# Expert projections of a mixture of experts: weights as the moving operand in plain float32, biases by matmul

## The reference, cut to what matters

```
logits = xt @ w_router + b_router            # 32 experts
top_v, top_i = top_k(logits, 4); gates = softmax(top_v)
# for every expert e, on the rows that chose it:
hdn  = xblk @ w1[e] + b1[e]                  # 1024 -> 2048
gate = minimum(hdn[:, :1024], 7.0)
lin  = clip(hdn[:, 1024:], -7.0, 7.0)
act  = gate * sigmoid(1.702 * gate) * (lin + 1.0)
yb   = act @ w2[e] + b2[e]                   # 1024 -> 1024
out[token] += gate_weight * yb
```

## Time and profile before

| what | value |
|---|---|
| median of three runs | 2697.32 us |
| span of the profiled execution | 2696.2 us |
| TensorE matmul busy | 2443.9 us (91%) |
| TensorE weight load busy | 1888.3 us (70%) |
| VectorE busy | 954.6 us (35%) |
| ScalarE busy | 631.2 us (23%) |
| mean granted TensorE clock | 0.941 |

### The profile page before, as it was taken

The page is one execution under the profiler, slowest core; times in us unless marked ns, Lnnn a source line. Parts: engine busy times, 40 slices in busy tenths (PEclk is TensorE's granted clock), DMA queues, the critical chain, the costliest instruction groups (busy, mean ns, idle before and its releaser), DMA issues. The chain is left out here.

```text
span 2696.2 us, 36055 instructions
## 1 busy us (share of the span) xinstructions
PE 2443.9 (91%) x14394; PEld 1888.3 (70%) x14394; DVE 954.6 (35%) x1243; ACT 631.2 (23%) x822; POOL 254.4 (9%) x179
## 2 busy tenths in 40 slices
PE   5799889987957899997899999999999999999991
PEld 3455456464725444475899999999999999999981
DVE  3332314464556000003133433434334243343335
ACT  3422203041322100001122322323223222232231
POOL 0000020324042000000000000000000000000000
PEclk8899899998976899996899999999999999999996
DMA  5111022313121422232588888888888888888854
GB/s 165 49 47 47 0 94 67 119 49 110 78 93 47 151 71 73 77 125 96 193 325 307 320 319 317 322 313 320 324 309 319 315 319 329 303 320 320 313 196 167
DMA packets 160137, 527.75 MB, mean 196 GB/s; under 512 B 15382, under 2 KB 81848, under 8 KB 124248
## 3 DMA queue, kind: packets, MB, share of 16 engines
q1 hardware_dynamic: 152808, 505.69, 51.8%
q0 software_dynamic: 7280, 21.37, 2.6%
HBM read 510.12 MB, written 21.10 MB: 197 GB/s over the span
## 5 line engine op out<-in xcount | busy, mean ns | idle before, releaser
L1619 PE MATMUL ps<-temps,weights 128*128 128x96 f32 x8192 | 925.2, 276 | 0.0
L1619 PEld LDWEIGHTS ps<-temps,weights 128*128 128x128 f32 x8192 | 920.9, 193 | 0.0
L1683 DVE TENSOR_TENSOR w_low<-weights,w_high 128x1024 fp32r<-128x1024 f32 x256 | 305.1, 1223 | 52.5 <-ACT w_high L1677 52.4
L1631 DVE TENSOR_TENSOR temps<-ps,b1T 128x768 f32<-128x768 f32 x64 | 58.4, 954 | 671.9 <-PE ps L1619 671.9
L1677 ACT ACTIVATE w_high<-weights 128x1024 fp32r<-128x1024 f32 x256 | 260.4, 1053 | 48.8 <-PE ps L1694 48.8
L1609 ACT ACTIVATE temps<-ps 128x384 f32<-128x384 f32 x66 | 28.9, 491 | 795.5 <-PE ps L1601 795.5
L1694 PE MATMUL ps<-w_high,act_high 128*96 128x512 f32 x512 | 204.2, 399 | 8.9 <-DVE w_low L1683 8.9
L1694 PE MATMUL ps<-w_high,act_low 128*96 128x512 f32 x512 | 201.5, 394 | 0.0
L1694 PE MATMUL ps<-w_low,act_high 128*96 128x512 f32 x512 | 200.8, 392 | 0.0
L1242 PE MATMUL ps<-weights 128*128 128x512 f32 x384 | 169.0, 600 | 5.1 <-PEq L1145 5.1
L850 PE MATMUL ps<-weights 128*128 128x512 f32 x384 | 169.7, 597 | 0.0
(11 more groups left out here) (280 smaller groups left out, 2248.8 us busy)
## 6 DMA issues: line engine op xcount, KB each, us to landing
weights<-in_w SPq DMA_DIRECT2D x384, 1024.0 KB, 5.8
weights<-in_w_in SPq DMA_DIRECT2D x32, 1024.0 KB, 5.4
weights<-in_w_in SPq DMA_DIRECT2D x16, 512.0 KB, 5.1
temps<-cum_rows SPq DMA_DIRECT2D x8, 1024.0 KB, 7.1
weights<-cum_rows SPq DMA_DIRECT2D x8, 1024.0 KB, 11.2
weights<-in_w_up_ssd SPq DMA_DIRECT2D x8, 1024.0 KB, 6.5
weights<-expert_rows SPq DMA_DIRECT2D x16, 512.0 KB, 10.0
ssd_out_T<-temps SPq DMA_DIRECT2D x4, 1024.0 KB, 3.9
```

The costliest lines, as they stand in the source:

```text
L1619: last = nc.tensor.matmul(ps[:, m // 4, (m % 4) * CAP:(m % 4 + 1) * CAP], slot(k, 1)[:, 0, m * P:(m + 1) * P], xeT[:, k, :], start=k == 0 ...
L1631: nc.vector.tensor_tensor(dst.rearrange("p (a c s) -> p a c s", a=2, c=4), ps[:, 2 * i:2 * i + 2, 0:4 * CAP].rearrange("p a (c s) -> p a c ...
L1683: nc.vector.tensor_tensor(w_lo[:, cols], src, w_hi[:, cols].bitcast(F32), ALU.subtract).then_inc(w_lo_ok, 1)
```

## The change

Both projections now use the transposed rows or activations (96 columns) as stationary operand and stream 512 columns of weights in plain float32. The splits of w2 and of the activations are gone, with their buffers. The hidden layer now has rows on partitions, so the bias differs along the free axis; it enters by four float32r matmuls of `pick` (a 0/1 matrix that selects row e and row 32 + e) with `b1_s` (b1's rounded part in rows 0 to 31, the rest in rows 32 to 63, zeros below). Activations need a transpose of their own (`acts_pe`). Sigmoid and product become one Silu with scale 1.702, and the factor 1/1.702 goes into a copy. The weights' store becomes one ring of 8 slots (`RING`) through which the 12 tiles of a pass go in the order of use. Index matmuls are float32r with two columns, four in place of eight, and stand inside the up projection. Gathered rows have two buffers, and slots and gathers run a pass further ahead.

```
-            for k in range(NK):
-                pe.wait_ge(exp_w[k], it * 16 + 16)
-                for m in range(2 * DFF // P):
-                    last = nc.tensor.matmul(ps[:, m // 4, (m % 4) * CAP:(m % 4 + 1) * CAP], slot(k, 1)[:, 0, m * P:(m + 1) * P], xeT[:, k, :], ...
-                last.then_inc(l1_used, 1)
+        def up_pe(pe, it, odd):
+            pe.wait_ge(x_ok, it + 1)
+            pe.wait_ge(pick_ok, it + 1)
+            if not is_first(it):
+                pe.wait_ge(gl_ok, it * 2)
+            for n in range(4):
+                nc.tensor.matmul(ps[0:CAP, n, :], pick[:, :], b1_s[:, n * 512:(n + 1) * 512], start=True, stop=False)
+            for k in range(UP):
+                at = ring_at(it, odd, k)
+                pe.wait_ge(exp_w[at], landed(it, odd, k))
+                for n in range(4):
+                    last = nc.tensor.matmul(ps[0:CAP, n, :], xT[:, k, :], slot(at, 1)[:, 0, n * 512:(n + 1) * 512], start=False, stop=k == UP - 1)
+                last.then_inc(w_used, 1)
+                if k == 2:
+                    if not is_first(it):
+                        pe.wait_ge(a_ok, it)
+                    slots_pe(pe, it + 2)
+        def slots_pe(pe, it):
+            pe.wait_ge(s_oh, it + 1)
+            for t in range(NT):
+                last = nc.tensor.matmul(ps[0:CAP, 6, 400:402], sel[:, t, :], slot_of[:, bass.ds((it % NE) * NT * 2 + t * 2, 2)], ...
+            last.then_inc(ix_ps, 1)
+        def gate_dve(v, it):
+            v.wait_ge(w_used, tile_no(it, UP - 1) + 1)
+            if not is_first(it):
+                v.wait_ge(aT_tp, it)
+            nc.vector.tensor_scalar(g_w[0:CAP, :]..., ps[0:CAP, 0:2, :], LIMIT, None, ALU.min).then_inc(gl_ok, 1)
+            nc.vector.tensor_scalar(l_w[0:CAP, :]..., ps[0:CAP, 2:4, :], LIMIT, -LIMIT, ALU.min, ALU.max).then_inc(gl_ok, 1)
+        def silu_act(act, it):
+            act.wait_ge(gl_ok, it * 2 + 1)
+            nc.scalar.activation(g_w[0:CAP, :], g_w[0:CAP, :], ACT.Silu, scale=ALPHA).then_inc(silu_ok, 1)
+        def glu_dve(v, it):
+            v.wait_ge(silu_ok, it + 1)
+            v.wait_ge(gl_ok, it * 2 + 2)
+            nc.vector.scalar_tensor_tensor(l_w[0:CAP, :], l_w[0:CAP, :], 1.0, g_w[0:CAP, :], ALU.add, ALU.mult).then_inc(glu_ok, 1)
+        def acts_pe(pe, it):
+            pe.wait_ge(glu_ok, it + 1)
+            pe.wait_ge(x_ok, it + 2)
+            for c in range(NK):
+                last = nc.tensor.transpose(ps[:, 6 + c // 4, ...], l_w[0:CAP, c * P:(c + 1) * P], ident[0:CAP, 0:CAP])
+            last.then_inc(aT_tp, 1)
+        def acts_act(act, it):
+            act.wait_ge(aT_tp, it + 1)
+            nc.scalar.activation(a_f[:, :]..., eighths(6), ACT.Copy, scale=1.0 / ALPHA).then_inc(a_ok, 1)
+        def down_pe(pe, it, odd, first):
+            pe.wait_ge(a_ok, it)
+            if not (isinstance(it, int) and it == 1):
+                pe.wait_ge(ye_ok, it - 1)
+            for u in range(DOWN):
+                at = ring_at(it, odd, first + u)
+                pe.wait_ge(exp_w[at], landed(it, odd, first + u))
+                for k in (2 * u, 2 * u + 1):
+                    for n in range(2):
+                        last = nc.tensor.matmul(ps[0:CAP, 4 + n, :], aT[:, k, :], slot(at, 2)[:, k % 2, n * 512:(n + 1) * 512], ...
+                last.then_inc(w_used, 1)
+        def pass_pe(pe, it, odd):
+            up_pe(pe, it, odd)
+            rows_pe(pe, it + 1, 1 - odd)
+            if not is_first(it):
+                down_pe(pe, it, odd, UP)
+            acts_pe(pe, it)
+        def pass_act(act, it):
+            if not is_first(it):
+                acts_act(act, it - 1)
+                if not (isinstance(it, int) and it == 1):
+                    down_act(act, it - 1, TILES, it * 16 - 32)
+            rows_act(act, it + 1)
+            silu_act(act, it)
+        def pass_dve(v, it):
+            if not is_first(it):
+                places_dve(v, it - 1)
+            tokens_dve(v, it + 2)
+            slots_dve(v, it + 3)
+            pick_dve(v, it + 1)
+            gate_dve(v, it)
+            glu_dve(v, it)
+        def load_tile(sp, it, odd, j):
+            sp.wait_ge(w_used, tile_no(it, j) - (RING - 1))
...
```

Here `down_pe(pe, it, ...)` in the new code works on the expert of pass it - 1. In the blocks before: the merge block loses the load, the four transposes (L1312) and the copy (L1371) of b1 and the preload of w2; the routing block gains two loads of b1, and these instructions (the first of them in VectorE's chain, the last three at its end):

```
+                then(nc.vector.tensor_copy(slots4[:, :, :, 0], tok_id.unsqueeze(2).broadcast_to([P, NT, NE])))
+                nc.scalar.activation(b1_s[0:2 * NE, :], b1_rows[0:2 * NE, :], ACT.Copy).then_inc(b1_hi, 1)
+                nc.vector.tensor_tensor(expert_at, ident[:, 0:NE], ident[:, NE:2 * NE], ALU.add).then_inc(b1_lo, 1)
+                nc.vector.memset(b1_s[2 * NE:P, :].bitcast(F32), 0.0).then_inc(b1_lo, 1)
+                nc.vector.tensor_tensor(b1_s[low_half, :], b1_rows[low_half, :], b1_s[low_half, :].bitcast(F32), ALU.subtract).then_inc(b1_lo, 1)
```

More of the change, by code:

```diff
@@ L49 @@
 FAR = 4096.0
+RING = 8
 UNIT = 2048
@@ L1378, in build, with sb_r @@
         rt_ps = sem("rt_ps")
-        take_anew()
+        b1_in = sem("b1_in")
+        b1_hi = sem("b1_hi")
+        b1_lo = sem("b1_lo")
+        before_experts.close()
+        def sb_r(name, cols):
+            return ctx.enter_context(nc.sbuf_tensor(name, [P, cols], F32R))
+        x_f, a_f = (sb(n, NK * CAP) for n in ("rows_T", "act_T"))
+        b1_s = sb_r("bias_split", 2 * DFF)
+        pick = sb_r("pick", CAP)
+        slot_of = sb_r("slot_of", 2 * NE * NT)
+        sel_r = sb_r("sel", NT * CAP)
+        take_anew()
+        gate = take(NT * TOPK).rearrange("p (t k) -> p t k", t=NT)
+        rank_m = take(NT * NE)
+        iota_r = take(SLOTS + CAP)
+        trips = take(2).bitcast(I32)
+        expert_at = take(NE)
+        after_route = used["main"]
         top_v = take(NT * 8).rearrange("p (t k) -> p t k", t=NT)
@@ L1400, in build @@
         trips_f = take(1)
-        trips = take(2).bitcast(I32)
-        after_route = used["main"]
+        assert used["main"] <= TEMPS - NT * D
         with nc.Block() as block:
@@ L1407, in _ @@
                 sp.dma_start(b2_w[0:NE, :], b2).then_inc(b_in, 16)
+                for half in range(2):
+                    sp.dma_start(b1_rows[half * NE:(half + 1) * NE, :], b1).then_inc(b1_in, 16)
             @block.gpsimd
@@ L1604, in rows_act @@
+            last.then_inc(xT_tp, 1)
         def rows_act(act, it):
-            act.wait_ge(xeT_ps, it + 1)
+            act.wait_ge(xT_tp, it + 1)
             if not is_first(it):
[L1607 to L1613, removed]
-            if not is_first(it):
-                pe.wait_ge(b1_add, it * 2)
-            for k in range(NK):
-                pe.wait_ge(exp_w[k], it * 16 + 16)
-                for m in range(2 * DFF // P):
-                    last = nc.tensor.matmul(ps[:, m // 4, (m % 4) * CAP:(m % 4 + 1) * CAP], slot(k, 1)[:, 0, m * P:(m + 1) * P], xeT[:, k, :],
-                                            start=k == 0 and m % 4 == 0, stop=k == NK - 1, skip_group_check=True)
-                last.then_inc(l1_used, 1)
@@ L1748, in _ @@
             def _(sp):
-                last, before = last_pass(sp), pass_before(sp)
-                load_w1(sp, 1)
-                with sp.Fori(2, last + 1, 2) as pair:
-                    for it in (pair, pair + 1):
-                        load_w1(sp, it)
-                        load_w2(sp, it - 1)
-                load_w2_last(sp, before)
+                end = after_last(sp)
+                for j in range(TILES):
+                    load_tile(sp, 1, 1, j)
+                with sp.Fori(2, end, 2) as pair:
+                    for odd in range(2):
+                        for j in range(TILES):
+                            load_tile(sp, pair + odd, odd, j)
@@ L1768, in _ @@
-                scatter_pool(pool, last)
-                pool.wait_ge(xe_in, last * 16 + 32)
-                pool.wait_ge(ye_out, last * 16 + 16)
+                end = after_last(pool)
+                for it in range(4):
+                    gather_pool(pool, it, it % 2)
+                with pool.Fori(2, end, 2) as pair:
+                    for odd in range(2):
+                        scatter_pool(pool, pair + odd - 2)
+                        gather_pool(pool, pair + odd + 2, odd)
+                scatter_pool(pool, end - 2)
@@ L1792, in _ @@
+                with pe.Fori(2, end, 2) as pair:
+                    for odd in range(2):
+                        pass_pe(pe, pair + odd, odd)
+                down_pe(pe, end, 0, 0)
             @block.scalar
             def _(act):
-                last, before = last_pass(act), pass_before(act)
+                end = after_last(act)
+                before = eng_before(act)
                 rows_act(act, 0)
-                rows_act(act, 1)
-                act_act(act, 0)
+                pass_act(act, 0)
@@ L1798, in _ @@
                 pass_act(act, 1)
-                with act.Fori(2, last + 1, 2) as pair:
-                    for it in (pair, pair + 1):
-                        pass_act(act, it)
-                split_act(act, last)
```

(26 more changed lines are left out.)

289 lines of the change are left out of this document (95 added, 194 removed).

## The result

| | before | after |
|---|---|---|
| median, us | 2697.65 (2697.01 to 2700.14, 4 runs) | 2766.18 (2765.41 to 2768.09, 4 runs) |
| ratio | 1 | 1.0253, 95% interval 1.0239 to 1.0268 |
| span of the profiled execution | 2696.2 | 2766.0 |
| VectorE, ScalarE busy | 954.6, 631.2 | 601.4, 375.5 |

The change makes the kernel 68.5 us slower; the forecast was 64.2. The two profiled executions differ by 69.8 us.

What follows compares the result with a forecast made beforehand. TensorE, busy throughout the experts' stage, was taken as the bound. Start -0.6, pass 0 +3.3, thirty full steps +62.7 and last pass -1.2 gave +64.2 us, a median of 2761.5 us, range 2744 to 2786.

Steps and rivals of the forecast that it cites:

- The bound: Experts' stage: a pass lasts the sum of TensorE's pieces, 41.69 us before and 43.78 after, 2.09 more.
- Up: Up projection per pass: 64 float32 records at 0.4292 make 27.47 us, 1.17 less than 28.64.
- Down: Down projection per pass: 32 float32 records at 0.4292 make 13.73 us, 2.59 more than 11.14.
- Biases, slots, transposes: TensorE's small matmuls per pass: biases 0.98 us, slots 0.38, transposes of rows and activations 0.61 each, 1.22 together.
- Hand-overs: Activations' chain to `acts_pe`, at most 4.7 us, and other engines' work stay hidden under transposes and down of 14.3.
- `up` of pass 0: Start of the experts' stage: the edges before it add up so that it begins about 0.6 us earlier.
- the last pass: End of the experts' stage: +2.8 us before the first down ends, -4.0 after it, together -1.2.
- A: TensorE's 512-column pass needs less than 0.429 a record with 96 stationary columns; faster from 0.407 on; chance 0.03.
- B: Weights arrive late through 8 slots: with flow held to 290 GB/s, pass 45.9 us, time 2829; chance 0.05.
- C: A hand-over, chain to `acts_pe` or type switches, is exposed in each pass: at 1 us each 2793; chance 0.07.
- D: TensorE's granted clock falls under continuous 512-column streaming: at a mean of 0.95, +74, 2835 us; chance 0.03.
- E: Terms cancel because slots and biases vanish under streaming and the edges win: no change; chance below 0.01.

Runs made afterwards that it cites:

- experiment 1: Changed kernel without its four bias matmuls per pass (b1 left out): 2734.18 us, 32.0 less than the changed kernel.
- experiment 2: Kernel before with only the down projection made one plain float32 matmul, no splits: 2775.77 us, +77.4, ratio 1.0289.
- experiment 3: Kernel before with only the new index matmuls (four float32r of two columns for eight float32 of one): 2662.20 us, ratio 0.9868.
- experiment 4: Changed kernel with half of the down matmuls left out (first 512 output columns only), all loads kept: 2542.39 us.
- experiment 6: Changed kernel with its four index matmuls issued twice in each pass, same result: 2774.83 us, +8.7.
- experiment 5: Changed kernel's layout with both projections split into three float32r matmuls, activations' transposes inside the next pass: 2523.04 us, ratio 0.9354 to the kernel before.

## Why the prediction was right, step by step

**The bound.** TensorE's sum set the pass before and after. Experiments 1 to 4 and 6 each changed one term, experiment 5 several, and each distance moved by the price of what was changed: 42.87 where 42.8 was expected, 44.34 (44.2 to 44.3), 40.67 (40.7 to 40.8), 36.92 (36.92), 36.08 (36 to 37), 44.14 (43.79 + 0.33 = 44.12).

**Up.** 27.80 with slots, where 27.47 + 0.38 stood. Streaming w1 was not tried alone. After is 9.6 faster than experiment 2, which shares its down, while the new slots alone gave 36.1 (experiment 3). So the rest of the change (streamed w1, biases, transposes of activations, the work on b1, the open hand-over of pass 0) costs 36.1 - 9.6, some 26, together. By the rows, 31 x (27.47 + 0.99 + 0.61 - 28.64) = 13 of them fall in the steady passes; the split of the rest is worked out, not shown by a run.

**Down.** 13.73 to the hundredth. This is the cause of the loss: experiment 2 alone costs 77 us, and experiment 5, which returns to float32r and extends it to w1, turns the loss into a gain. The argument for 0.429 with 96 stationary columns was thinner than it reads: the block of rows 6 has fewer rows (32) but the same 128 columns as rows 5, so neither tested fewer columns. The 13.73 of after does.

**Biases, slots, transposes.** 0.99 (0.98 stood), 0.33 by the sum (0.38), and 0.66 + 0.61 (1.22). The slots came out 0.05 lower and the row transposes 0.05 higher, so that the sum meets 43.79 to 0.01 is in part luck. Experiments 1 and 6 put the net prices at 0.92 and 0.35. Two bounds of the biases were reckoned wrong: without the change of type 4 x 0.231 is 0.92, not 0.85, and 1.72 is the price of one float32 record a matmul, where rows 5 have two. The range did not hang on either.

**Hand-overs.** None shows in a steady pass. They are open only where no down hides them: the transposes of activations of pass 0 wait 4.53 (at 1335.66), the last down 1.99 (at 2698.91). In the timeline of VectorE around the end of an up projection of after, the clamps and the product are done 4.1 us after 2024.81, and the transposes that need them start at 2039.20:

```profile
2025.01 1.22 DVE L1677 TENSOR_SCALAR temps<-ps 96x1024 f32<-96x1024 f32 x1 [15.87 <-PE ps L1665]
2026.15 1.21 DVE L1678 TENSOR_SCALAR temps<-ps 96x1024 f32<-96x1024 f32 x1
2027.64 1.22 DVE L1689 SCALAR_TENSOR_TENSOR temps<-temps 96x1024 f32<-96x1024 f32 x1 [0.28 <-ACT temps L1683]
```

**Where the 4 us between 64.2 and 68.5 are.** Only the profiled executions can be taken apart, and there the difference is 69.8, 5.6 more than forecast. In them `up` of pass 0 (with its biases) starts at 1299.18 where 1296.21 stood, +3.0 in place of -0.6; pass 0 takes 37.7 (37.0 stood); the thirty next together +63.6 (62.7); the last pass -0.4 (-1.2), and what follows it -0.3 (0). The first is the term that was off, by 3.6. The routing block itself came as reckoned (from 34.2 to 39.2, +4.9 stood), and the way from there to `up` became 4.7 shorter (4.1 stood). But the merge stage's L1293 began 0.9 later, and from there to the end of L1305 it took 3 us longer in this execution, though the change does not touch these matmuls:

```profile
1168.61 55.52 PE L1293 MATMUL ps<-weights,temps 128*128 128x256 f32 x256 [1.70 <-DVE temps L1344]
1229.68 6.65 PE L1299 MATMUL ps<-ident,side_temps 128*128 128x128 f32 x32 [5.54 <-DVE side_temps L1360]
1237.53 12.36 PE L1305 MATMUL ps<-temps,side_temps 128*128 128x32 f32 x64 [1.21 <-ACT side_temps L1331]
```

The execution of experiment 1, whose code is the same up to here, has 5.21 and 10.69 for the last two, as before does, and its `up` of pass 0 starts at 1296.37. The gap before them is 5.54 or 5.55 in all three, and in all three the granted clock is down at 0.50 (1.2 GHz) when the matmuls start again. What differs is how late it rises and how soon it falls again. The same stretch of before, then of after:

```profile
1232.00:1234.00 2.00, 1.95 (x18) 1.72 (x16) 0.27 (x1) 1.76 (x2) 0.00 (x0) 1.00 1.02 287
...
1232.00:1234.00 2.00, 2.00 (x12) 2.00 (x11) 1.21 (x2) 1.32 (x2) 0.00 (x0) 0.50 1.03 430
```

So some 3 of the 5.6 us differ from execution to execution and are not a cost of the change; why the clock rises later in some of them no run shows. The other executions of after were 1.4 to 2.7 us shorter and not profiled; how much of the 4.3 us between the medians and the forecast is the same effect stays open.

**The rivals.** A fell: the records of 96 stationary columns run at 0.429 (32 in 13.73). B fell by experiments 4 and 5: 358 and 368 GB/s through 8 slots. (The 325 to 328 GB/s of rows 2 are two stretches; the mean of before over 1200 us is 317.) C fell by the rows above. D fell: the clock is 1.00 over all 1200 us. E fell: the kernel is slower by 2.5%, with an interval of 2.4 to 2.7%. The Trainium skill ("TensorE: Matmul & The Clock Gate", section "Back-to-back issue gap") gives 216 ns for an isolated matmul of 512 columns and 131 ns for one in a sustained stream. The streams here are near the first: 0.231 for a float32r matmul, and 0.429 / 2 = 0.215 if a float32 record stands for two of the four passes that the prediction counts. The 131 ns is in none of them.

## What to carry to other kernels

When TensorE is busy for all of a stage and the others aren't, price every matmul by its pace in a stream and add. Work saved on engines that nobody waits for counts nothing. With 512 moving columns, a split into three float32r matmuls (0.69) beats one float32 matmul (0.858) as long as ScalarE and VectorE have the time. When a change bundles parts, price each alone: here a gain of 36 us sat inside a loss of 68. If the sum shows that one choice of type loses, work out the opposite choice for all of the work too.

## What the runs showed of the hardware that I had not expected

In experiment 5 the DMA engines moved 368 GB/s over 1000 us at a share of 0.98, and no engine waits for a DMA in that stretch. Flow over share was 356 in after (303 at 0.85), 370 in experiment 3 (326 at 0.88), 369 in experiment 4 (358 at 0.97) and 376 in experiment 5. So a limit scaled up from a stretch at 0.85 came out some 5% low: I had put it at 352.

Four float32r matmuls of two columns, put into a stream of float32 ones, seem to cost 0.69 at the spot. Of this, 0.41 is given back by the records before them (24 take 9.89 from the first start to the change, 10.30 by their pace), and the 40 behind them take 0.05 more than their pace. The net is 0.33.

The same code after the same gap of TensorE ran its next 96 records in 5.21 + 10.69 = 15.9 us in six of the eight profiled executions, and in 6.65 + 12.36 = 19.0 in the other two (after and experiment 6; each to 0.03). In the slower ones the granted clock stayed at 0.50 longer after the gap.
